# A hybrid encoder step: last tiles' squares summed by TensorE, middle r chain moved ahead, spreads inside a product, one entry's high part moved

## The chip, the cores and the metric

One core of a Trainium2 chip runs the whole step. The metric is the device time of one execution in microseconds (us); lower is better. Engine names below: PE is TensorE, DVE is VectorE, ACT is ScalarE, POOL is GpSimd, SP is SyncE, which issues nearly all DMAs.

## The reference

One step of a two-layer streaming encoder on 1,024 prompt frames and 32 sample frames (1,056 columns in all), with a model width of 1,024.

```python
def rmsnorm(x, g):
    xf = x.astype(jnp.float32)
    y = xf * lax.rsqrt(jnp.mean(xf * xf, axis=-1, keepdims=True) + EPS)
    return (y * g.astype(jnp.float32)).astype(x.dtype)
...
    for l in range(DEPTH):                       # DEPTH = 2
        h = rmsnorm(x, norm_mix[l])
        ...                                      # mixer A/B (l = 0) or mixer C (l = 1)
        x = x + y
        h = rmsnorm(x, norm_ffn[l])
        y, pf = conv_ffn(h, past_f[l], w_up[l], conv_f_w[l], w_down[l])
        new_f.append(pf)
        x = x + y
    return rmsnorm(x, norm_final), ...
```

What matters here is rmsnorm: each frame's mean square over 1,024 channels gives a factor r = (mean square + EPS)^(-1/2), which multiplies that frame's column.

## The kernel before

**Layout.** Activations lie transposed: x is 8 tiles of 128 channels by 1,056 frames (x_t[:, m, :], m = 0 to 7). So a sum over channels is a sum over 8 tiles and then over 128 partitions. Every fp32 product is made of three fp32r matmuls (split_product, lines 694 to 696): weights and activations are each split into a high part (a copy rounded by ACT) and a low part (the difference, made by POOL for weights and by DVE for activations).

**Stages.** After the first mixer come stages p = 1, 2, 3 (FFN, mixer C, FFN). A stage starts while the down products of the one before still end (last_down(p) on ACT, DVE and POOL): tile by tile x gets its residual (DVE), is scaled and split, and squared. The stage's first product is first_pair(p). It uses weight entries of 128 x 512: entries 0 and 1 for its first group (weights(0), weights(1)), 2 and 3 later. Each entry needs its high part from ACT (entry_hi, line 1417) and then its low part from POOL (entry_lo, line 1191). The products run on unnormalised x; r is applied to results. The r chain is: squares summed over tiles (sumsq), 128 partitions summed by PE against a column of ones (rms_stats), mean square on DVE (lines 1948, 1949), the power -1/2 on POOL (r_col, line 1220), spread over partitions by PE as transposes of a broadcast column (rms_spread, line 766), copied to r_rows by ACT (line 1673).

**The end.** The last down product (unit LAST) is cut into 3 chunks of columns: 0 to 400, 400 to 800 and 800 to 1,056. In each, PE makes 8 tiles of 6 matmuls. DVE adds each to x (chunk_add, line 2565), ACT squares it (end_squares_of, line 1859), and the squares are summed: chunk 0 by POOL and DVE, chunks 1 and 2 by DVE one tile at a time in PSUM (part_squares, line 2595), the last sum being written to sumsq. chunk_stats sums partitions (line 1125), chunk_mean_square (line 2572), chunk_r on POOL (line 1369), chunk_spread (line 1136) and copy_r (line 1841) follow, for chunks 0 and 1 amid the products of the next chunk. chunk_y multiplies a tile of x by r: on POOL (line 1378) in the order of POOL_Y, on DVE (line 2584) in the order of DVE_Y. Chunk 2 goes out untransposed instead: its 8 tiles are turned by PE (line 1172, 16 transposes, 2 for each tile) and scaled by r_col as they leave PSUM, half by ACT (line 1884) and half by DVE (line 2626). Both engines' halves wait for end_turned, which the last transpose raises.

**Order.** Every engine runs a list written out by hand, with waits on semaphores. SP issues the stores in the order of Y_STORES: (c, first, end) is tiles first to end - 1 of chunk c (200 KB a tile), ("act", t) and ("dve", t) are the quarters of chunk 2 (256 KB each). A store waits for its data, and all stores behind it wait too.

## Time and profile before

| | us |
|---|---|
| median of 3 runs (2094.25 to 2094.81) | 2094.79 |
| the profiled execution, its own time | 2094.42 |
| its span | 2092.6 |
| PE busy | 2080.4 |
| DVE, POOL, ACT busy | 1509.2, 964.5, 747.1 |

The profile counts time from the start of its span; 1.8 us of the execution's own time lie outside the span. Busy times overlap between engines, and a busy PE can hold matmuls that are pipelined into one another: a matmul's listed length is longer than the distance to the next one's start. Lost PE time is therefore read from start to start.

### The profile page before, as it was taken

The numbers are of one execution on the slowest core, as the hardware profiler recorded it, in microseconds if no ns is written. First come the engines' busy times: TensorE is split into PE (matmuls) and PEld (weight loads), VectorE is DVE, ScalarE is ACT, GpSimd is POOL, SyncE is SP. The second block draws the span as 40 slices with busy tenths as digits, with TensorE's granted clock in tenths as the row PEclk, the third lists the DMA queues.
The fourth block names the chain that finished last, engine by engine and source line by source line (L and its number), as shares of the span: only waits on it lengthen the run. The fifth ranks groups of instructions, "written<-read, shape, count | busy, mean of one in ns | idle before, by whom it ended". The sixth has DMA issues, their size and how long they took to land.

```text
span 2092.6 us, 36500 instructions
## 1 busy us (share of the span) xinstructions
PE 2080.4 (99%) x15414; PEld 2072.4 (99%) x15414; DVE 1509.2 (72%) x1843; ACT 747.1 (36%) x1158; POOL 964.5 (46%) x610
## 2 busy tenths in 40 slices
PE   9999999999999999999999999999999999999998
PEld 9999999999999999999999999999999999999998
DVE  6999689766666667666987677798676666766666
ACT  6574354233222322223532223453322233222234
POOL 3867335444443444443565345455444344444344
PEclk9999999999999999999999999999999999999999
DMA  4111211111111110111111111111111111011112
GB/s 167 52 33 68 99 61 42 61 61 41 41 54 49 62 51 31 61 41 61 41 41 62 41 61 41 61 41 61 41 41 61 41 61 51 31 61 42 61 43 89
DMA packets 34036, 115.66 MB, mean 55 GB/s; under 512 B 3985, under 2 KB 6545, under 8 KB 33873
## 3 DMA queue, kind: packets, MB, share of 16 engines
q1 hardware_dynamic: 33728, 112.78, 16.1%
q8 instruction: 122, 2.00, 0.4%
q10 hardware_dynamic: 144, 0.54, 0.1%
q14 instruction: 42, 0.34, 0.1%
HBM read 108.69 MB, written 4.62 MB: 54 GB/s over the span
## 4 chain that ended last, share of the span: by engine, by line
PE 93%; DVE 3%; issue 1%; POOL 1%; ACT 0%; DMA 0%; POOLq 0%; DVEq 0%; ACTq 0%
PE psum L694 31%; PE psum L696 31%; PE psum L695 30%; DVE xs_lo L1969 1%; DVE xs_lo L2209 1%; DVE work L2247 1%; DVE r_rows L2236 1%; POOL x L1378 0%; PE psum L823 0%; DVE work L2249 0%; DVE x L1936 0%; PE psum L766 0%; POOL r_col L1220 0%; DMA raw<-slabs 0%; PE psum L848 0%
## 5 line engine op out<-in xcount | busy, mean ns | idle before, releaser
L694 PE MATMUL psum<-xs_hi,w_hi 128*128 128x264 f32 (+2 forms) x3784 | 1101.5, 291 | 1.1 <-POOL w_lo L1191 0.5
L696 PE MATMUL psum<-xs_hi,w_lo 128*128 128x264 f32 (+2 forms) x3784 | 1100.0, 291 | 0.0
L695 PE MATMUL psum<-xs_lo,w_hi 128*128 128x264 f32 (+2 forms) x3784 | 1096.4, 290 | 0.0
L1191 POOL TENSOR_TENSOR w_lo<-raw,w_hi 128x512 fp32r<-128x512 f32 (+1 forms) x412 | 663.9, 1623 | 822.8 <-ACT w_hi L1417 740.5
L694 PEld LDWEIGHTS psum<-xs_hi,w_hi 128*128 128x128 f32 x3784 | 711.8, 188 | 3.3 <-issue 1.3
L695 PEld LDWEIGHTS psum<-xs_lo,w_hi 128*128 128x128 f32 x3784 | 711.3, 188 | 0.0
L696 PEld LDWEIGHTS psum<-xs_hi,w_lo 128*128 128x128 f32 x3784 | 711.2, 188 | 0.0
L694 PE MATMUL psum<-act_hi,w_hi 128*128 128x352 f32 x1200 | 388.3, 324 | 0.1
L696 PE MATMUL psum<-act_hi,w_lo 128*128 128x352 f32 x1200 | 388.2, 323 | 0.0
L695 PE MATMUL psum<-act_lo,w_hi 128*128 128x352 f32 x1200 | 385.4, 321 | 0.0
L1417 ACT ACTIVATE w_hi<-raw 128x512 fp32r<-128x512 f32 x383 | 234.0, 625 | 289.6 <-PE psum L696 268.8
L1933 DVE TENSOR_TENSOR x<-psum,x 128x704 f32<-128x704 f32 x200 | 177.8, 889 | 148.7 <-PE psum L696 143.4
L695 PEld LDWEIGHTS psum<-act_lo,w_hi 128*128 128x128 f32 x1200 | 227.4, 190 | 0.0
L694 PEld LDWEIGHTS psum<-act_hi,w_hi 128*128 128x128 f32 x1200 | 225.0, 188 | 1.1 <-issue 0.7
L696 PEld LDWEIGHTS psum<-act_hi,w_lo 128*128 128x128 f32 x1200 | 224.9, 187 | 0.0
L1965 DVE SCALAR_TENSOR_TENSOR work<-work,const 128x1058 f32<-128x1058 f32 x104 | 165.7, 1593 | 2.3
L1198 POOL TENSOR_TENSOR w_lo<-raw,w_hi 128x512 fp32r<-128x512 f32 x44 | 68.0, 1545 | 164.5 <-ACT w_hi L1404 164.5
L1706 ACT ACTIVATE work<-work 128x1024 f32<-128x1024 f32 x41 | 43.6, 1063 | 193.3 <-DVE work L1965 193.3
L1404 ACT ACTIVATE w_hi<-raw 128x1024 fp32r<-128x1024 f32 x52 | 55.1, 1059 | 160.5 <-PE psum L696 160.5
L1698 ACT ACTIVATE act_hi<-work 128x1056 fp32r<-128x1056 f32 x40 | 43.3, 1082 | 189.1 <-PE psum L696 189.1
L2444 DVE TENSOR_TENSOR work<-psum,work 128x528 f32<-128x528 f32 x53 | 37.4, 705 | 96.7 <-PE psum L696 96.7
L1936 DVE TENSOR_TENSOR x<-psum,x 128x352 f32<-128x352 f32 x200 | 102.5, 513 | 0.0
(242 smaller groups left out, 1851.0 us busy)
## 6 DMA issues: line engine op xcount, KB each, us to landing
raw<-slabs SPq DMA_DIRECT2D x186, 512.0 KB, 3.3
x<-x_t SPq DMA_DIRECT2D x15, 528.0 KB, 6.0
y_t<-x SPq DMA_DIRECT2D x4, 400.0 KB, 2.9
y_t<-x SPq DMA_DIRECT2D x8, 200.0 KB, 2.1
raw<-slabs SPq DMA_DIRECT2D x4, 256.0 KB, 8.2
y_end<-y_rows SPq DMA_DIRECT2D x4, 256.0 KB, 2.9
x<-x_t ACTq DMA_DIRECT2D x1, 528.0 KB, 4.7
x<-mix SPq DMA_DIRECT2D x1, 512.0 KB, 3.4
```

The source lines that it names most:

```text
L694: nc.tensor.matmul(out, w_hi[:, w], hi, start=start, stop=False, skip_group_check=reopen)
L695: nc.tensor.matmul(out, w_hi[:, w], lo, start=False, stop=False, skip_group_check=reopen)
L696: return nc.tensor.matmul(out, w_lo[:, w], hi, start=False, stop=stop, skip_group_check=reopen)
L1191: nc.gpsimd.tensor_tensor(w_lo[:, slab], src, w_hi[:, slab].bitcast(F32), ALU.subtract).then_inc(weights_ready, 1)
L1198: nc.gpsimd.tensor_tensor(w_lo[:, a], src[:, 0:ENTRY], w_hi[:, a].bitcast(F32), ALU.subtract)
L1404: nc.scalar.activation(w_hi[:, ring(p, unit, i)], raw_at(n), ACT.Copy).then_inc(weights_hi, 1)
L1417: nc.scalar.activation(w_hi[:, ring(p, unit, i)], entry(p, b, q, i), ACT.Copy).then_inc(weights_hi, 1)
L1698: nc.scalar.activation(ah[slot], prod[q], ACT.Copy).then_inc(act_hi_ready, 1)
L1706: nc.scalar.activation(f[:, 0:SEQ], conv_out[:, 0:SEQ], ACT.Silu)
L1933: first = dve.tensor_tensor(wide(x_t[:, m, :]), wide_banks(pset), wide(x_t[:, m, :]), ALU.add)
L1936: dve.tensor_tensor(x_t[:, m, chunk(2)], rest_bank(pset), x_t[:, m, chunk(2)], ALU.add).then_inc(tile_evacuated, 1)
L1965: dve.scalar_tensor_tensor(out, conv_in[:, k:k + GAP_COLS], cst(w_name, w_at + k), out, ALU.mult, ALU.add).then_inc(conv_tap, 1)
```

## The change

Four edits, and a new order of stores:

1. **Last tiles' squares.** In chunk 2, DVE adds up the squares of tiles 0 to 3 alone (END_SUMMED = 4), in place of all 8. PE sums the partitions of that total and then of the squares of tiles 4, 5, 6 and 7, accumulating all five in the same two PSUM columns (end_stats). The transposes of tile 0 come between tile 6's and tile 7's sums, and the other transposes after them. end_turned is now raised twice, after tile 3 (for ACT) and after tile 7 (for DVE).
2. **Middle part's r chain.** In chunk 1, DVE takes the mean square ahead of a sum of squares. POOL takes chunk 1's r after 6 tiles of y in place of 7, and chunk 2's r after 10 in place of 11. PE spreads chunk 1's r before tile 5 of chunk 2 in place of tile 6. ACT copies it before tile 4's square in place of tile 5's. DVE makes its first two tiles of y between the last additions.
3. **Spreads within a product.** rms_spread stands 3 matmuls later, inside the product that followed it, in stages 1 to 3. chunk_spread(0) stands 3 matmuls later too, between the two halves of chunk 1's tile 4.
4. **One entry's high part.** In stage 1, ACT makes entry 0's high part before tile 5's scaled copy in place of after its square, apart from entry 1's.

```diff
-Y_STORES = ((0, 4, 6), (0, 6, KD), (0, 0, 2), (0, 2, 3), (0, 3, 4), (1, 4, 5), (1, 0, 1), (1, 5, 6), (1, 1, 3), (1, 6, 7),
-            (1, 3, 4), ("act", 0), ("act", 1), ("dve", 0), (1, 7, KD), ("dve", 1))
+Y_STORES = ((0, 4, 6), (0, 6, KD), (0, 0, 2), (0, 2, 3), (1, 0, 1), (0, 3, 4), (1, 4, 5), (1, 1, 2), (1, 5, 6), (1, 2, 3),
+            (1, 3, 4), ("act", 0), (1, 6, 7), ("dve", 0), ("act", 1), ("dve", 1), (1, 7, KD))
+END_SUMMED = 4
...
                 pe.wait_ge(part_copied, 3 * n + 3)
+                block_product(a22, X_B22, x_bank, 0, False, False, halves=(0,))
                 rms_spread(p, psum[:, Y_BANK, 300:300 + ROW_REST])
-                for kp in range(KP):
+                block_product(a22, X_B22, x_bank, 0, False, False, halves=(1,))
+                for kp in range(1, KP):
                     last = block_product(a22, X_B22, x_bank, kp, False, kp == KP - 1)
...
+            def end_stats(squares, opens, closes):
+                for t, (at, rows) in enumerate(FINAL_ROWS[2]):
+                    n = 8 + t
+                    last = nc.tensor.matmul(psum[0:rows, 7, n:n + 1], squares[:, at:at + rows],
+                                            one[:], start=opens and t == 0, stop=closes, skip_group_check=True)
+                return last
...
-                    if c and m == (4, 6)[c - 1]:
-                        chunk_spread(c - 1)
+                    if (c, m) == (2, 5):
+                        chunk_spread(1)
...
+                        if (c, m, k) == (1, 4, 1):
+                            chunk_spread(0)
...
-            last.then_inc(end_turned, 1)
-            chunk_stats(2)
+            pe.wait_ge(part_summed, KD - 1 + END_SUMMED - 1)
+            end_stats(sumsq, True, False)
+            for m in range(END_SUMMED, KD - 1):
+                pe.wait_ge(square_ready, KD * 6 + m + 1)
+                end_stats(end_square[m], False, False)
+            pe.wait_ge(tile_evacuated, FINAL_EVAC + 2 * KD + 6)
+            end_turn(0)
+            pe.wait_ge(square_ready, KD * 7)
+            end_stats(end_square[KD - 1], False, True).then_inc(stats_ready, 1)
+            for m in (1, 2):
+                end_turn(m)
+            end_turn(3).then_inc(end_turned, 1)
+            pe.wait_ge(tile_evacuated, FINAL_EVAC + 3 * KD)
+            for m in (4, 5, 6):
+                end_turn(m)
+            end_turn(7).then_inc(end_turned, 1)
...
             chunk_r(0)
-            chunk_y(0, 7)
+            chunk_y(0, 6)
             chunk_r(1)
-            chunk_y(7, 11)
+            chunk_y(6, 10)
             chunk_r(2)
-            chunk_y(11, len(POOL_Y))
+            chunk_y(10, len(POOL_Y))
...
+                    if p == 1 and m == 5:
+                        entry_hi(p, 0, 0, 0)
...
-                    if m == 5:
+                    if m == 5 and p == 1:
+                        entry_hi(p, 0, 0, 1)
+                    elif m == 5:
                         entry_hi(p, 0, 0, 0, 1)
...
             for m in range(KD):
-                if m == 5:
+                if m == 4:
                     copy_r(1)
                 end_squares_of(2, m)
-                if m in (2, 4):
-                    scale(1, 5 + m // 2)
-                elif m in (0, 1, 3, 5):
-                    end_scale((m + 1) // 2)
+                if m == 2:
+                    scale(1, 6)
+                elif m in (0, 1, 3, 4):
+                    end_scale(m if m < 2 else m - 1)
+            scale(1, 7)
...
                 if m == 0:
                     part_squares(1, KD - 1)
-                elif m >= 2:
-                    part_squares(2, m - 1)
-                if m == 2:
+                elif m == 2:
                     chunk_mean_square(1)
-            part_squares(2, KD - 1)
-            chunk_y(1, 0, 1)
+                    part_squares(2, 1)
+                elif m == 4:
+                    part_squares(2, 2)
+                    chunk_y(1, 0, 1)
+                elif m == 5:
+                    part_squares(2, 3)
+            chunk_y(1, 1, 2)
             chunk_mean_square(2)
-            chunk_y(1, 1, 4)
-            dve.wait_ge(end_turned, 1)
+            chunk_y(1, 2, 4)
+            dve.wait_ge(end_turned, 2)
```

How the order of instructions moves, at three places (line numbers of the changed kernel are a little higher).

PE at the end of the program, before: after the last product (L696) stand 16 transposes of x (L1172; 4 of the 8 pairs shown) and then the partition sums of sumsq (here named r_rows, which shares its buffer; one is the column of ones).

```order
L696 MATMUL psum<-xs_hi,w_lo 128x256
L1172 MATMUL psum<-ident,x 128x128 [waits tile_evacuated,end_scaled]
L1172 MATMUL psum<-ident,x 128x128
...
L1172 MATMUL psum<-ident,x 128x128 [waits tile_evacuated]
L1172 MATMUL psum<-ident,x 128x128
L1125 MATMUL psum<-one,r_rows 128x1 [waits part_summed]
L1125 MATMUL psum<-one,r_rows 128x1
```

PE at the same place, in the changed kernel (L1135 is end_stats, L1146 the transposes):

```order
L697 MATMUL psum<-xs_hi,w_lo 128x256
L1135 MATMUL psum<-one,r_rows 128x1 [waits part_summed]
L1135 MATMUL psum<-one,r_rows 128x1
L1135 MATMUL psum<-one,end_squares 128x1 [waits square_ready]
L1135 MATMUL psum<-one,end_squares 128x1
...
L1146 MATMUL psum<-ident,x 128x128 [waits end_scaled,tile_evacuated]
L1146 MATMUL psum<-ident,x 128x128
L1135 MATMUL psum<-one,end_squares 128x1 [waits square_ready]
L1135 MATMUL psum<-one,end_squares 128x1
L1146 MATMUL psum<-ident,x 128x128 [waits end_scaled]
...
L1146 MATMUL psum<-ident,x 128x128 [waits tile_evacuated]
```

Two sums and 16 transposes became ten sums, of which eight come before any transpose, two transposes, the last two sums, and 14 transposes.

DVE in chunk 2, before, from the third addition (L2565) on; L2595 is a sum of squares, L2572 a mean square, L2584 a tile of y:

```order
L2565 TENSOR_TENSOR x<-psum,x 128x256 [waits tile_evacuated,tile_done] x2
L2595 TENSOR_TENSOR psum<-psum,end_squares 128x256 [waits square_ready]
L2572 TENSOR_SCALAR mean_sq<-psum 100x4 [waits stats_ready]
L2565 TENSOR_TENSOR x<-psum,x 128x256 [waits tile_evacuated,tile_done]
...
L2595 TENSOR_TENSOR r_rows<-psum,end_squares 128x256 [waits part_summed,square_ready]
L2584 SCALAR_TENSOR_TENSOR x<-x,const,psum 128x400 [waits r_ready,r_spread]
L2572 TENSOR_SCALAR mean_sq<-psum 128x2 [waits stats_ready]
L2584 SCALAR_TENSOR_TENSOR x<-x,const,psum 128x400 [waits r_ready,r_spread]
```

DVE at the same place, in the changed kernel (L2595 is now the addition, L2625 a sum of squares, L2602 a mean square, L2614 a tile of y):

```order
L2595 TENSOR_TENSOR x<-psum,x 128x256 [waits tile_evacuated,tile_done] x2
L2602 TENSOR_SCALAR mean_sq<-psum 100x4 [waits stats_ready]
L2625 TENSOR_TENSOR psum<-psum,end_squares 128x256 [waits square_ready]
L2595 TENSOR_TENSOR x<-psum,x 128x256 [waits tile_evacuated,tile_done] x2
L2625 TENSOR_TENSOR psum<-psum,end_squares 128x256 [waits part_summed,square_ready]
L2614 SCALAR_TENSOR_TENSOR x<-x,const,psum 128x400 [waits r_ready,r_spread]
L2595 TENSOR_TENSOR x<-psum,x 128x256 [waits tile_evacuated,tile_done]
L2625 TENSOR_TENSOR r_rows<-psum,end_squares 128x256 [waits part_summed,square_ready]
L2595 TENSOR_TENSOR x<-psum,x 128x256 [waits tile_evacuated,tile_done] x2
L2614 SCALAR_TENSOR_TENSOR x<-x,const,psum 128x400 [waits r_ready,r_spread]
L2602 TENSOR_SCALAR mean_sq<-psum 128x2 [waits stats_ready]
```

Seven sums of squares became three; the first tile of y stands before the last three additions and the second right behind them.

## Rows read from the trace of the kernel before

**Rows 1.** The page, busy time of each engine.
```profile
PE 2080.4 (99%) x15414; PEld 2072.4 (99%) x15414; DVE 1509.2 (72%) x1843; ACT 747.1 (36%) x1158; POOL 964.5 (46%) x610
```

**Rows 2.** Busy time by stage: us, each engine's busy time, PEclk, DMA share, GB/s.
```profile
2082.00:2093.00 11.00, 2.07 (x19) 1.87 (x17) 4.96 (x11) 2.10 (x5) 4.18 (x5) 0.71 0.67 250
```

**Rows 3.** Timeline of PE: spreads of stages 1 and 3 (start, us).
```profile
333.18 0.28 PE L696 MATMUL psum<-xs_hi,w_lo 128*128 128x264 f32 x1
333.63 1.23 PE L766 MATMUL psum<-ident,r_col 128*128 128x128 f32 x9 [0.18 <-POOL r_col L1220]
...
1389.86 0.28 PE L696 MATMUL psum<-xs_hi,w_lo 128*128 128x264 f32 x1
1390.34 1.23 PE L766 MATMUL psum<-ident,r_col 128*128 128x128 f32 x9 [0.20 <-POOL r_col L1220]
```

**Rows 4.** Timeline of POOL ahead of stage 1's spread.
```profile
329.67 1.58 POOL L1305 TENSOR_TENSOR xs_lo<-work,xs_hi 128x528 fp32r<-128x528 f32 x1 [4.45 <-ACT xs_hi L1654]
331.22 2.27 POOL L1220 TENSOR_TENSOR r_col<-mean_sq,minus_half 128x9 f32<-128x9 f32 x1
```

**Rows 5.** Timeline of PE, POOL, ACT and DVE where stage 1 starts.
```profile
309.92 0.32 PE L696 MATMUL psum<-xs_hi,w_lo 128*128 128x352 f32 x1
310.74 0.36 PE L694 MATMUL psum<-xs_hi,w_hi 128*128 128x264 f32 x1 [0.49 <-POOL w_lo L1191]
...
307.32 3.16 POOL L1191 TENSOR_TENSOR w_lo<-raw,w_hi 128x512 fp32r<-128x512 f32 x2 [2.77 <-ACT w_hi L1417]
...
306.62 1.14 ACT L1417 ACTIVATE w_hi<-raw 128x512 fp32r<-128x512 f32 x2
...
309.23 2.36 DVE L2209 SCALAR_TENSOR_TENSOR xs_lo<-x,const,xs_hi 128x1056 fp32r<-128x1056 f32 x1
```

**Rows 6.** Timeline of PE in the last two chunks and behind.
```profile
2069.41 0.34 PE L696 MATMUL psum<-xs_hi,w_lo 128*128 128x400 f32 x1
2069.90 0.56 PE L1136 MATMUL psum<-ident,r_col 100*128 100x100 f32 x4
...
2081.68 1.91 PE L1172 MATMUL psum<-ident,x 128*128 128x128 f32 x16
2083.47 0.61 PE L1125 MATMUL psum<-one,r_rows 128*128 128x1 f32 x4
```

**Rows 7.** Timeline of DVE behind chunk 1's products.
```profile
2078.49 0.15 DVE L2572 TENSOR_SCALAR mean_sq<-psum 100x4 f32<-100x4 f32 x1
...
2082.09 0.41 DVE L2565 TENSOR_TENSOR x<-psum,x 128x256 f32<-128x256 f32 x1
...
2084.11 0.16 DVE L2572 TENSOR_SCALAR mean_sq<-psum 128x2 f32<-128x2 f32 x1 [0.16 <-PE psum L1125]
2084.19 1.71 DVE L2584 SCALAR_TENSOR_TENSOR x<-x,const,psum 128x400 f32<-128x400 f32 x3
```

**Rows 8.** Timeline of ACT and POOL in the same stretch.
```profile
2080.92 0.48 ACT L1841 ACTIVATE r_rows<-psum 128x400 f32<-128x400 f32 x1
...
2071.07 7.12 POOL L1378 TENSOR_TENSOR x<-x,r_rows 128x400 f32<-128x400 f32 x7 [1.23 <-ACT r_rows L1841]
2078.72 1.01 POOL L1369 TENSOR_TENSOR r_col<-mean_sq,minus_half 128x4 f32<-128x4 f32 x1 [0.52 <-DVE mean_sq L2572]
...
2081.48 3.04 POOL L1378 TENSOR_TENSOR x<-x,r_rows 128x400 f32<-128x400 f32 x3 [0.74 <-ACT r_rows L1841]
2084.46 0.72 POOL L1369 TENSOR_TENSOR r_col<-mean_sq,minus_half 128x2 f32<-128x2 f32 x1
```

**Rows 9.** Timeline of SP's queue: stores (1, 1, 3) and ("dve", 1).
```profile
2085.39 0.38 SPq L685 DMA_DIRECT2D y_t<-x  x1
...
2089.34 0.64 SPq L676 DMA_DIRECT2D y_end<-y_rows  x1
```

**Rows 10.** Busy time in quarters of a us; the last two columns are DMA share and GB/s.
```profile
2086.25:2086.50 0.25, 0.00 (x0) 0.00 (x0) 0.25 (x2) 0.25 (x1) 0.00 (x0) 1.00 0.78 294
...
2091.50:2091.75 0.25, 0.00 (x0) 0.00 (x0) 0.00 (x0) 0.00 (x0) 0.00 (x0) 0.50 0.85 328
```

More of the change, by code:

```diff
@@ L924, in _, with block_product @@
                 last.then_inc(tile_done, 1)
[L926 to L928 removed]
+            def block_product(slab, which, first_bank, kp, opens, closes, reopen=False, halves=(0, 1)):
+                for h in halves:
                     at = kp * KP_COLS + which + h * PART
@@ L1127, in chunk_stats, with end_turn @@
                 last.then_inc(stats_ready, 1)
+            def end_stats(squares, opens, closes):
[4 more added lines that the diff above has]
+                return last
+            def end_turn(m):
+                if m < 4:
+                    pe.wait_ge(end_scaled, m + 1)
+                    bank = END_BANKS["act"]
+                else:
+                    bank = END_BANKS["dve"]
+                for t in range(END_ROWS):
+                    last = nc.tensor.transpose(psum[:, bank[t], m % 4 * P:(m % 4 + 1) * P],
+                                               x_t[:, m, END + t * P:END + (t + 1) * P], ident[:])
+                return last
             def chunk_spread(c):
```

18 lines of the change are left out of this document (2 added, 16 removed).

## The prediction, made before the changed kernel ran

> **What bounds the kernel now.** I read the page first: PE is busy for 2080.4 of 2092.6 us [rows 1], so all that any change off PE can win is 12.2 us. I then went through PE's timeline for places where one matmul starts later than the usual distance behind the last. Inside the program these are few and small. At each of the three spreads of r the first transpose starts 0.45 to 0.48 us behind a matmul whose followers come every 0.12 us [rows 3]; that is 0.33 us lost in stage 1 and 0.36 in stage 3, and 0.27 in stage 2, the one of the three not shown. Stage 1's first product starts 0.66 us late (0.82 us behind the last one, where 0.16 is usual), put down to a weight's low part on POOL [rows 5]. The spread of chunk 0 starts 0.49 us behind, where 0.18 is usual: 0.31 us lost [rows 6].
>
> The rest lies behind the last product, where PE is busy 2.07 of 11 us [rows 2]. There I asked what ends last. It is the stores: the DMA engines move 294 GB/s from 2086.25 on, are nearly full from then (the last quarter of a microsecond still has 328), and stop before 2091.75 [rows 10]. By the shares of those two quarters (0.78, 0.85) data flow from 2086.27 to 2091.71. SP issued the store that opens this stretch at 2085.39 [rows 9], 0.88 us before its data move. From it to the last there are 400 + 200 + 200 + 256 + 256 + 256 + 200 + 256 = 2,024 KB = 2.073 MB, in 5.44 us: 381 GB/s. The span ends 0.89 us later. So the end is not a chain of engines but a full DMA path, and the rule that I use is: the end is, over all stores, the latest of (issue + 0.88 + bytes from this store on / 381 GB/s), plus 0.89. What counts is how early the data before the last ones leave, not when the last tile is ready.
>
> **The spreads within a product.** Three matmuls at 0.12 us are put ahead of each rms_spread: 0.36 us of cover. What the spread waits for is r_col, which POOL ends at 331.22 + 2.27 = 333.49 [rows 4]; the transposes begin 0.14 us behind. Nothing in the edit moves r_col, so the spread stays where it is and the three matmuls are won: 0.33, 0.27 and 0.36, which is 0.96 us. Behind the spread ACT copies r as before, and PE comes to the next pair 0.36 us earlier with no wait listed there. If r_col were later by some d, as much would be lost again; if all cover came to nothing, the term is 0. I take -0.96.
>
> **The moved entry.** Before, ACT makes both high parts from 306.62 on and POOL both low parts from 307.32 to 310.48, 1.2 to 1.6 us each [rows 5]. The high part of entry 0 (0.57 us) now falls in a gap of ACT. POOL could make its low part up to 2.7 us earlier. Yet I count nothing for it, for two reasons. First, what the 0.66 us win, the spread gives back: r_col of stage 1 stands behind POOL's xs_lo at 329.67, which had waited 4.45 us for ACT [rows 4]; ACT in turn waited for DVE, whose list has no gap from the start of stage 1 to there. PE would only wait longer at the spread. Second, DVE and POOL hinder each other. The DVE row at 309.23 ends 2.36 us later, at 311.59, 1.11 us behind POOL's two [rows 5]: as if it had stood still until POOL was through, for 1.25 us. So each of POOL's subtractions can push DVE's chain, and with it r_col, by about that. Before, one does. After, by the order of requests the total may be the same (0), and at worst both do: 1.25 us later. I take 0, and keep 0 to +1.3.
>
> The Trainium skill, "SBUF — State Buffer", section "Who interferes with whom", says that a DVE instruction with two SBUF inputs and a GpSimd instruction that reads SBUF exclude each other for the whole length of whichever issued first. The row of 2.36 us agrees. By that rule alone an earlier POOL subtraction would come ahead of DVE's and hold it up, which is the first rival below.
>
> **The last chunks, PE and DVE up to the additions.** Times are on the clock of before; only differences inside the end count. chunk_spread(0) costs no wait any more: PE is 0.31 us earlier from there on, and DVE, which follows it tile by tile, too. Chunk 1's r: its stats end near 2077.4. The mean square then stands first on DVE (2077.45, for 2078.49 [rows 7]). POOL has ended six tiles by then (seven took 7.12 us, so 1.02 each [rows 8]), and r_col lasts 1.01 from 2077.7. So r is there at 2078.7 for 2079.73, PE spreads before tile 5, and ACT's copy starts at 2079.8 for 2080.92 [rows 8], where its list now comes to it. r_rows is ready at 2080.3 for 2081.4. DVE's first y waits for that (2080.31), and holds up the additions of tiles 5 to 7. From 2080.31 on DVE is full: 0.55 to the next instruction behind a y, 0.34 behind an addition or a sum. So tile 5's addition starts at 2080.86, the last sum of squares at 2081.20, tile 6's and 7's additions at 2081.55 and 2081.9, the last for 2082.09 [rows 7]. The two lost waits and the one new one nearly cancel.
>
> **PE's sums.** The total of tiles 0 to 3 is written at 2081.63 on DVE (2081.20 + 0.43). A sum is four records on PE's timeline, where two matmuls stand in the program [rows 6]. From 2083.47 those four take 0.61, of which 0.25 is the last one's own length, so 0.12 a record; 16 transposes in 1.91 are 0.11 each. Nine of ten matmuls now read squares that are already there, so PE runs at its own pace: 20 records x 0.11 + 2 x 0.11 for tile 0's transposes, from 2081.69 on, is 2084.1, and the last result 0.2 later. The mean square of chunk 2 starts at 2084.3 for 2084.11 [rows 7]. So this edit takes four additions (0.35 each) and a wait from DVE, but puts 2.4 us of PE into the chain, and r of chunk 2 is not earlier: 2085.25 for 2085.18 [rows 8]. The six transposes of tiles 1 to 3 end before that, those of tiles 4 to 7 at 2085.8: ACT writes its quarters as before, DVE too (2085.87, for 2085.82 which is 0.08 before the end of its y [rows 7]).
>
> **y and the stores.** POOL after r: chunk 0's last two to 2080.7, chunk 1's tiles 4 and 5 end at 2081.75 and 2082.75 (before, 2082.5 and 2083.5 [rows 8]). It then waits for chunk 2's mean square until 2084.5, and ends tile 6 at 2086.3 and tile 7 at 2087.3, the latter 1.1 us later than before. DVE ends tiles 0 and 1 at 2080.95 and 2082.85, and, behind the mean square (2084.4), tile 2 at 2085.0 and tile 3 at 2085.55 (three of them in 1.71, so 0.62 each and 0.55 apart [rows 7]). SP's last wait before the path fills is tile 2 of chunk 1: issued at 2085.03, with 200 + 200 + 256 + 200 + 256 + 256 + 256 + 200 = 1,824 KB = 1.868 MB from there on. 2085.03 + 0.88 + 4.90 = 2090.81. Tile 3: 2085.58 + 0.88 + 4.36 = 2090.82. ("act", 0): 2086.06 + 0.88 + 3.83 = 2090.77. Tile 7, though last and late, is issued long after it is ready. Data end at 2090.82 for 2091.71: -0.89 us.
>
> The Trainium skill, "DMA: Bandwidth & Descriptors", section "Where 436 GB/s comes from", puts transfers between HBM and SBUF at about 358 GB/s. The trace shows 381 with one core running, and the measurement decides; by 358 the same two sums would be 5.79 and 5.22 us of data, and the term -0.93 instead of -0.89.
>
> **Sum.** -0.96 (spreads) + 0 (entry) - 0.89 (stores) = -1.85 us. PE's 0.31 us of chunk 0 is inside the second. Against the profiled execution: 2094.42 - 1.85 = 2092.57. The median of the runs shown is 0.37 above it: 2094.79 - 1.85 = 2092.9.
>
> **Rivals.** A measurement of this kernel tells about 0.2% (4.2 us) from no change; of faster and slower in that sense nearly nothing is in reach, since all of PE's losses in the program are 2.1 us and the end's can't fall below its bytes.
> - *The moved entry delays r of stage 1.* DVE is blocked by both subtractions: +1.3 on r_col, so stage 1 gives +1.0 in place of -0.33. Time: 2092.9 + 1.3 = 2094.2. For it: the row of 2.36 us. Against: POOL asks back to back, and the two are likelier to take the same slots as before. 0.08.
> - *The stores win nothing.* POOL's idle 1.8 us before r of chunk 2, or DVE's y behind PE's sums, moves the opening store back: 2085.03 becomes 2085.9. Only the spreads are left: 2094.79 - 0.96 = 2093.8. 0.14.
> - *The spreads win nothing,* as the wait comes back at another place, or the switch between transposes and product was the gap: 2094.79 - 0.89 = 2093.9. For it: the profile itself puts only 0.18 and 0.20 of the gaps down to r_col [rows 3]. 0.07.
> - *Slower.* Ten sums in a row into the same two PSUM columns no longer pipeline. Every 0.1 us more per record adds 2.0 us ahead of chunk 2's mean square and of DVE's tiles 2 and 3, thus to the end. At 0.20 a record the store term is +0.9 and cancels the spreads; at 0.25 (a record's whole length) it is -0.89 + 2.8 = +1.9, and the kernel takes 2094.79 - 0.96 + 1.9 = 2095.7. Against: the four records of before already add into the same columns at 0.12. 0.05.
> - *More than forecast.* The sums go faster than DVE's old chain, or the copy of r finds ACT free earlier, and the opening store leaves 0.6 to 1.2 us earlier: 2091.7 to 2092.3. 0.12.
> - *As forecast,* within 0.7 us: 0.54.
>
> **The numbers.** All cases but part of the slower one and of the last lie between 2091.4 and 2094.6; this leaves out under 0.2 even with the runs' own spread (0.56 us). 0.2% below is 2090.6: I give it 0.04, as losses of 4.2 us are hardly there to be won. 0.2% above is 2099.0: 0.02. Within: 0.94.
>
> **What would show it.** In the changed trace: the spreads start within 0.2 us of their neighbours, at the same distance behind r_col, and each stage is about 0.3 us earlier; the first product of stage 1 starts late as before or the spread waits longer; the mean square of chunk 2 at the same distance from the last product as before or a little more; POOL idle for over 1 us before chunk 2's r; data end 0.9 us nearer to PE's last product plus 0.3. Wrong would be: a DVE chain in stage 1 that is longer by over a microsecond, a record of the sums over 0.15 us, or a DMA path that is not full in the last 4 us.

## The result and the profile after

| | us |
|---|---|
| before, median of 19 runs (2094.05 to 2095.35) | 2094.52 |
| changed, median of 19 runs (2097.01 to 2099.71) | 2097.98 |
| ratio, 95% interval | 1.0017 (1.0011 to 1.0023) |
| profiled execution, its span | 2095.6 (before 2092.6) |

The kernel is 3.5 us slower, outside the range of the prediction (2091.4 to 2094.6), though within the 0.2% that it had called the bound of no change. The page of the changed kernel, its line of busy times:

```profile
PE 2082.2 (99%) x15430; PEld 2073.8 (99%) x15430; DVE 1511.7 (72%) x1839; ACT 747.0 (36%) x1158; POOL 967.1 (46%) x610
```

Against [rows 1] that says nothing: a stall of 1 us drowns in it. What tells is the distance from one matmul's start to the next on PE's timeline. In the changed kernel it shows a later start of stage 1, and three waits that the kernel before does not have, one in each stage, 19 to 31 us behind the spread of r. PE of the changed kernel at the start of stage 1, at its spread, and at the three waits:

```profile
309.94 0.32 PE L697 MATMUL psum<-xs_hi,w_lo 128*128 128x352 f32 x1
311.59 0.39 PE L695 MATMUL psum<-xs_hi,w_hi 128*128 128x264 f32 x1 [1.33 <-DVE x L1966]
...
334.42 0.28 PE L697 MATMUL psum<-xs_hi,w_lo 128*128 128x264 f32 x1
334.72 1.25 PE L767 MATMUL psum<-ident,r_col 128*128 128x128 f32 x9
...
353.00 0.29 PE L697 MATMUL psum<-xs_hi,w_lo 128*128 128x264 f32 x1
354.36 0.39 PE L695 MATMUL psum<-xs_hi,w_hi 128*128 128x264 f32 x1 [1.08 <-ACT work L1799]
...
1077.89 0.28 PE L697 MATMUL psum<-xs_hi,w_lo 128*128 128x264 f32 x1
1078.69 0.39 PE L695 MATMUL psum<-xs_hi,w_hi 128*128 128x264 f32 x1 [0.52 <-ACT work L1769]
...
1411.25 0.29 PE L697 MATMUL psum<-xs_hi,w_lo 128*128 128x264 f32 x1
1412.52 0.39 PE L695 MATMUL psum<-xs_hi,w_hi 128*128 128x264 f32 x1 [0.99 <-ACT work L1799]
```

The first product starts 0.85 us later than in [rows 5] (311.59 for 310.74), the spread 1.09 us later than in [rows 3] (334.72 for 333.63). The spread itself no longer waits much (0.30 us behind its neighbour for 0.45). Then come starts 1.36, 0.80 and 1.27 us apart where 0.12 is usual. The spreads of stages 2 and 3 start at 1047.56 and 1393.00, for 1045.42 and 1390.34 before: the loss grows from stage to stage. From the start of the last product (2084.70, before 2081.56) to the span's end it is 10.90 us for 11.04, so nearly nothing is won at the end.

Why stage 1 starts late, in the changed kernel: POOL (L1216 are the low parts of entries 0 and 1), and DVE from tile 5 on:

```profile
304.53 2.31 POOL L1216 TENSOR_TENSOR w_lo<-raw,w_hi 128x512 fp32r<-128x512 f32 x1
307.34 1.84 POOL L1216 TENSOR_TENSOR w_lo<-raw,w_hi 128x512 fp32r<-128x512 f32 x1 [0.49 <-ACT w_hi L1442]
...
305.61 2.42 DVE L1999 TENSOR_TENSOR xs_lo<-work,xs_hi 128x528 fp32r<-128x528 f32 x2
307.96 2.35 DVE L2266 TENSOR_TENSOR r_rows<-r_rows,work 128x1056 f32<-128x1056 f32 x1
310.23 0.88 DVE L1963 TENSOR_TENSOR x<-psum,x 128x704 f32<-128x704 f32 x1
311.03 0.51 DVE L1966 TENSOR_TENSOR x<-psum,x 128x352 f32<-128x352 f32 x1
311.46 1.30 DVE L2239 SCALAR_TENSOR_TENSOR xs_lo<-x,const,xs_hi 128x1056 fp32r<-128x1056 f32 x1
```

ACT's high part did fall into its gap (303.28), and POOL's low part starts 2.8 us earlier. But now both of POOL's subtractions fall on DVE instructions that read and write SBUF: L1999 takes 2.42 us and L2266 2.35. In the kernel before, the same two took 1.31 and 1.25, and one instruction alone was held up, the 2.36 us of [rows 5], which is now free at 1.30. Two blocks of about 1.1 us for one: DVE reaches the addition of tile 6 (L1963) 2.2 us later, PE waits for it, and r_col comes 1.17 us later (POOL starts on it at 332.39, for the 331.22 of [rows 4]).

### The profile page after: what moved, and what is told of

It is laid out like the page before. It is cut to its first block, busy times and chain, and to the rows that moved or that the text cites. A ratio compares the mean times of both kernels' runs of the same rounds, so it can differ in the third digit from the quotient of the medians.

```text
span 2095.6 us, 36523 instructions
## 1 busy us (share of the span) xinstructions
PE 2082.2 (99%) x15430; PEld 2073.8 (99%) x15430; DVE 1511.7 (72%) x1839; ACT 747.0 (36%) x1158; POOL 967.1 (46%) x610
## 4 chain that ended last, share of the span: by engine, by line
PE 88%; DVE 8%; issue 2%; POOL 1%; ACT 1%; DMA 0%; SPq 0%; DVEq 0%; ACTq 0%
PE psum L695 29%; PE psum L697 29%; PE psum L696 29%; DVE xs_lo L1999 2%; DVE xs_lo L2239 1%; DVE work L2277 1%; DVE r_rows L2266 1%; DVE work L1995 1%; DVE work L2279 0%; DVE x L1966 0%; PE psum L824 0%; DMA x<-x_t 0%; POOL r_col L1245 0%; DVE raw L2230 0%; POOL xs_lo L1330 0%
## 5 line engine op out<-in xcount | busy, mean ns | idle before, releaser
L696 PE MATMUL psum<-xs_lo,w_hi 128*128 128x264 f32 (+2 forms) x3784 | 1096.2, 290 | 0.0
L1216 POOL TENSOR_TENSOR w_lo<-raw,w_hi 128x512 fp32r<-128x512 f32 (+1 forms) x412 | 666.2, 1630 | 823.8 <-ACT w_hi L1442 741.7
L696 PEld LDWEIGHTS psum<-xs_lo,w_hi 128*128 128x128 f32 x3784 | 711.3, 188 | 0.0
L696 PE MATMUL psum<-act_lo,w_hi 128*128 128x352 f32 x1200 | 385.4, 321 | 0.0
L1963 DVE TENSOR_TENSOR x<-psum,x 128x704 f32<-128x704 f32 x200 | 177.8, 889 | 148.5 <-PE psum L697 143.3
L696 PEld LDWEIGHTS psum<-act_lo,w_hi 128*128 128x128 f32 x1200 | 227.4, 189 | 0.0
```

What stands on the lines that cost most here:

```text
L696: nc.tensor.matmul(out, w_hi[:, w], lo, start=False, stop=False, skip_group_check=reopen)
L1216: nc.gpsimd.tensor_tensor(w_lo[:, slab], src, w_hi[:, slab].bitcast(F32), ALU.subtract).then_inc(weights_ready, 1)
L1963: first = dve.tensor_tensor(wide(x_t[:, m, :]), wide_banks(pset), wide(x_t[:, m, :]), ALU.add)
```

## The experiments

Twelve kernels, and then, since the tail was still open, two more and four further executions of two of them. Every median stands beside the kernel before on the same chip: k_spread, k_entry, k_tail and k_noentry beside 2094.64; k_spread_swap, k_spread_silu, k_entry_late and k_r_early beside 2094.43; k_after_swap, k_after_fix, k_tail_stores and k_best beside 2094.40; the last two beside 2094.63. Kernels are compared by their distances to it. Each interval of a ratio is about 0.0009 to either side, so single differences under 2 us lie inside it; I read them by medians of 11 runs, their ranges, and the traces.

### The parts alone

**k_spread.** rms_spread inside the product, and nothing else:

```diff
+                block_product(a22, X_B22, x_bank, 0, False, False, halves=(0,))
                 rms_spread(p, psum[:, Y_BANK, 300:300 + ROW_REST])
+                block_product(a22, X_B22, x_bank, 0, False, False, halves=(1,))
-                for kp in range(KP):
+                for kp in range(1, KP):
```

> The kernel before with rms_spread inside the product (edit 3's first half) alone. Theory A: as forecast, the three spreads lose their waits, -0.96 us, 2093.5, and no wait of over 0.5 us behind any of them. Theory B: the copy of r and PE's second pair shift against DVE and POOL, and PE waits about 1 us for ACT's copy of a result in each stage, 353.0, 1077.9 and 1411.2 on the clock of the changed kernel: 3 waits of 0.5 to 1.2 us less the 0.96 won, thus 2095 to 2096.5.

Measured: 2097.06 (2096.75 to 2097.54), +2.42. Theory A, my forecast, falls, and the loss is larger than theory B's too; the largest part of the whole loss is here. DVE and POOL of this kernel behind the spread of stage 1:

```profile
337.83 1.22 DVE L2309 TENSOR_TENSOR work<-work,r_rows 128x1024 f32<-128x1024 f32 x1
338.97 1.28 DVE L2311 TENSOR_TENSOR work<-work,r_rows 128x32 f32<-128x32 f32 x1
340.17 1.31 DVE L2314 TENSOR_TENSOR work<-psum,r_rows 128x528 f32<-128x528 f32 x2
341.40 5.84 DVE L1971 TENSOR_TENSOR xs_lo<-slots_hi,xs_hi 128x528 fp32r<-128x528 f32 x4
...
338.68 1.53 POOL L1193 TENSOR_TENSOR w_lo<-raw,w_hi 128x512 fp32r<-128x512 f32 x1 [2.11 <-ACT w_hi L1419]
341.33 3.02 POOL L1193 TENSOR_TENSOR w_lo<-raw,w_hi 128x512 fp32r<-128x512 f32 x2 [1.13 <-ACT w_hi L1419]
```

The same engines in the kernel before:

```profile
338.63 0.18 DVE L2309 TENSOR_TENSOR work<-work,r_rows 128x32 f32<-128x32 f32 x1
338.73 1.32 DVE L2312 TENSOR_TENSOR work<-psum,r_rows 128x528 f32<-128x528 f32 x2
339.97 3.66 DVE L1969 TENSOR_TENSOR xs_lo<-slots_hi,xs_hi 128x528 fp32r<-128x528 f32 x4
...
338.74 1.30 POOL L1191 TENSOR_TENSOR w_lo<-raw,w_hi 128x512 fp32r<-128x512 f32 x1 [2.51 <-ACT w_hi L1417]
341.40 4.62 POOL L1191 TENSOR_TENSOR w_lo<-raw,w_hi 128x512 fp32r<-128x512 f32 x3 [1.36 <-ACT w_hi L1417]
```

Before, DVE's product of 32 columns was ahead of POOL's subtraction by 0.11 us (338.63, 338.74). PE's matmuls release the entry that ACT and then POOL take, so with PE 0.36 us nearer to the r chain POOL comes first (338.68, 338.97), and 0.18 us of work take 1.28.

The four low parts of t1 meet POOL's next subtractions, and three of the four take 1.79 us each. Before, only one of them did (1.80), but two DVE instructions behind them were held up instead, new_f (128x4, 1.26 us for 0.16) and L1961 (1.68 for 0.77); the convolution is held up once in both. Each kernel makes five POOL subtractions in this stretch; before, the first one fell on DVE instructions that read PSUM and cost nothing, here all five cost DVE 0.9 to 1.1 us. So the net loss is one block. From the 1,024-column product to the end of the convolution (L1965, there L1967) DVE needs 13.91 us (337.83 to 351.74) for 12.82 (337.50 to 350.32).

Stages 2 and 3 show the same: DVE's 32-column product was ahead of POOL by 0.10 us in each before (1050.42 for 1050.52, 1395.34 for 1395.44), is behind it now (1051.71 for 1051.56, 1397.26 for 1396.94), and takes 1.28 us both times. In stages 1 and 3 ACT's silu waits for the convolution, ACT's copy out of PSUM (L1772) stands behind silu, and PE waits for the copy; in stage 2 the copy (L1742) waits for DVE itself.

The waits account for the time. A stalled matmul starts 1.37 us behind the last for 0.12, and the one after it 0.23 for 0.12: 1.36 us in stages 1 and 3, by the same rows 0.81 in stage 2, together 3.53. Less 0.96 for the covered spreads it is +2.57; the span without what differed ahead of stage 1 (2095.5 - 0.33 - 2092.6) gives +2.57 as well.

**k_entry.** Edit 4 alone:

```diff
+                    if p == 1 and m == 5:
+                        entry_hi(p, 0, 0, 0)
                     act.wait_ge(tile_evacuated, read(m))
```

> The kernel before with edit 4 alone (entry 0's high part ahead of tile 5's scaled copy). Theory A, the moved entry starts the loss: POOL's two subtractions now hold up DVE twice for about 1.2 us where one did, so stage 1's first product starts 0.85 us later, r_col of stage 1 is 1.2 us later than before, and since the spread stands in its old place the whole of it is lost: 1.2 us, perhaps 1 more where later waits open, thus 2095.7 to 2096.7 beside a kernel before of 2094.5. Theory B, the spreads inside a product are at fault and the entry is harmless: 2094.5.

Measured: 2095.37 (2095.15 to 2095.66), +0.73. PE starts stage 1 at 311.50, and waits again at its spread, 334.72 with 0.47 us put down to r_col. Theory A's mechanism holds; the loss is smaller than the 1.2 to 2.2 us that it gave.

**k_tail.** Edits 1 and 2, the stores and chunk_spread(0).

> The kernel before with edits 1 and 2, the order of stores and chunk_spread(0) three matmuls later, but neither the moved entry nor rms_spread's new place. From the last product's start to the span's end the changed kernel took 10.9 us for 11.04: if that holds without the delays ahead of it, this gives -0.14 us, and with chunk_spread(0) -0.45: 2094.0 to 2094.4. The forecast's own term was -0.89, 2093.6. If the tail's edits carried part of the loss, it lies above 2094.8.

Measured: 2094.37 (2093.54 to 2096.12), -0.27, and 2.6 us wide for 1.0 before. The profiled execution has 2093.54, 0.88 us under that of before, which is the forecast's own number; but not all of it is the tail's. It is 0.34 us ahead already where chunk 0 begins, in front of everything that these edits touch. The first product of chunk 0 in the kernel before, and in k_tail:

```profile
2055.77 0.34 PE L694 MATMUL psum<-xs_hi,w_hi 128*128 128x400 f32 x1
```

```profile
2055.43 0.34 PE L695 MATMUL psum<-xs_hi,w_hi 128*128 128x400 f32 x1
```

From this product to the end of the span k_tail takes 36.3 us for 36.8. That distance is the measure of the tail: the six profiled kernels without any of its edits lie within 0.01 us of one another in it. So the tail gave -0.6 here, 0.4 of it ahead of the last product's start and 0.2 behind it.

**k_noentry.** The changed kernel without edit 4.

> The changed kernel with edit 4 undone. Theory A: r_col of stage 1 is back where it was, all three spreads are covered, -0.96 and the tail's -0.14 to -0.9: 2092.7 to 2093.4. Theory B: about the changed kernel's time less the 0.2 that the entry costs: 2097 to 2098.

Measured: 2097.18 (2096.27 to 2098.37). The three waits stand as in k_spread (1.08, 0.53 and 1.09 us idle; there 1.08, 0.54, 1.08). The parts nearly add: 2.42 + 0.73 - 0.27 = 2.88 of 3.5.

### Is it the race with POOL?

**k_spread_swap.** k_spread, and DVE takes the short product first:

```diff
-                dve.tensor_tensor(g[:, 2:2 + SEQ], g[:, 2:2 + SEQ], r_rows[:, 0:SEQ], ALU.mult).then_inc(tile_evacuated, 1)
                 sample = g[:, 2 + SAMPLE + GAP:2 + GAP_COLS]
                 dve.tensor_tensor(sample, sample, r_rows[:, SAMPLE:COLS], ALU.mult).then_inc(tile_evacuated, 1)
+                dve.tensor_tensor(g[:, 2:2 + SEQ], g[:, 2:2 + SEQ], r_rows[:, 0:SEQ], ALU.mult).then_inc(tile_evacuated, 1)
```

> rms_spread inside the product in stages 1 to 3, and DVE's two products with r behind it in the other order: the 32 columns first, then the 1,024. Theory P (a lost race with POOL): in the run with the spread alone, POOL's subtraction at 338.68 came ahead of the 32-column product, which took 1.28 us for 0.18, and the one at 341.33 ahead of four subtractions, which took 5.84 us for 3.66. With the long product last DVE is busy when POOL asks, so the 32 columns are not held up, DVE's chain is 1 to 2 us shorter, and PE's waits at 353.6 and 1411.9 shrink or go: 2094.3 to 2095.5 for 2097.06. Theory Q (PE is simply 0.36 us nearer to a chain that did not move): nothing changes but the order, 2097.0.

Measured: 2093.98 (2093.54 to 2094.36), 0.45 under before where k_spread is 2.42 above it. DVE and POOL of this kernel in the same place:

```profile
337.90 0.18 DVE L2310 TENSOR_TENSOR work<-work,r_rows 128x32 f32<-128x32 f32 x1
338.01 1.22 DVE L2311 TENSOR_TENSOR work<-work,r_rows 128x1024 f32<-128x1024 f32 x1
...
338.71 1.68 POOL L1193 TENSOR_TENSOR w_lo<-raw,w_hi 128x512 fp32r<-128x512 f32 x1 [2.07 <-ACT w_hi L1419]
```

POOL asks at the same moment, but DVE is amid its long instruction, so this time POOL stands (1.68 us, the longest of its first subtraction in the three kernels) and DVE's chain is 12.82 us again (337.90 to 350.72). PE's three waits are gone from the list of waits. Theory P holds: two instructions exchanged, with the same work, are worth 2.9 us. At 352.56 PE still starts 0.32 us behind its neighbour: ACT's copy starts at 351.92 and PE 0.64 later, as it did in k_spread (352.94, 353.58). By the same distance the kernel before had 0.25 us of slack there (copy at 351.51, PE on time at 352.40), less than the 0.36 won at the spread.

**k_spread_silu.** k_spread, with ACT's copy (L1770 of before) ahead of silu in stages 1 and 3:

```diff
-                if p != 2 and before == FIRST:
-                    silu_gate(p, 0, 0)
                 act.wait_ge(tile_done, group_done(p, b, q, 3))
...
                 nc.scalar.activation(two(half(up, 1)), halves_of(Z_BANK), ACT.Copy).then_inc(part_copied, 1)
+                if p != 2 and before == FIRST:
+                    silu_gate(p, 0, 0)
```

> rms_spread inside the product in stages 1 to 3, and in stages 1 and 3 ACT copies the first pair's fourth group out of PSUM before it computes silu of the first gate, in place of after. If PE's waits of 1.08 us in stages 1 and 3 (353.6, 1411.9; 1.25 from start to start) are for that copy standing behind silu, which stands behind DVE's convolution, they go, though POOL still holds up DVE: 2097.06 less 2.5 is 2094.6, of which the wait of 0.54 in stage 2 is left. If DVE or a low part is just as late, the wait stays with another name: above 2096.

Measured: 2096.44 (2096.16 to 2096.86), +2.01, so only 0.4 better than k_spread. The copy now starts at 349.51 and PE no longer waits for it, but PE stops 2.5 us later, at 356.04, idle for 0.73 us, put down to DVE (work, L2446), and likewise at 1413.84. DVE and POOL of k_spread there, and then of k_spread_silu:

```profile
353.68 0.71 DVE L2441 TENSOR_TENSOR work<-work,r_rows 128x528 f32<-128x528 f32 x1
354.13 3.68 POOL L1193 TENSOR_TENSOR w_lo<-raw,w_hi 128x512 fp32r<-128x512 f32 x2 [4.78 <-ACT w_hi L1419]
```

```profile
353.56 1.81 DVE L2441 TENSOR_TENSOR work<-work,r_rows 128x528 f32<-128x528 f32 x1
353.51 2.98 POOL L1193 TENSOR_TENSOR w_lo<-raw,w_hi 128x512 fp32r<-128x512 f32 x2 [4.28 <-ACT w_hi L1419]
```

It is the same race, lost at a new place. With its copy out of the way ACT makes the next two high parts 0.6 us earlier (352.82 for 353.43), POOL's subtraction starts 0.05 us ahead of DVE's product with r, and that product takes 1.81 us for 0.71; in stage 3 the starts are 1411.31 and 1411.36. L2446, which PE waits for, stands right behind it. Had the product taken 0.71 us, L2446 would have ended near 354.9 (an estimate: 1.1 us off its end at 355.98), ahead of PE's turn at 355.14. So the copy was rightly named as what PE waited for, and moving it moved POOL onto DVE once more.

**k_entry_late.** k_entry, with POOL's first low part held back until both high parts are there:

```diff
                 for i in entries:
+                    if (p, b, q, i) == (1, 0, 0, 0):
+                        pool.wait_ge(weights_hi, step_of(p, ("pair", b, q), 1) + 1)
                     split_lo(step_of(p, ("pair", b, q), i), ring(p, ("pair", b, q), i), entry(p, b, q, i))
```

> The kernel before with edit 4, but POOL starts entry 0's low part only when entry 1's high part is there too, as in effect before. ACT's order is that of the moved entry, POOL's times are those of before. Theory A (the loss of 0.73 us comes through POOL's early subtraction, which holds DVE up twice): back to 2094.6. Rival (ACT's own order is the cause, since tile 5's scaled copy comes 0.57 us later): 2095.4, as with edit 4 alone.

Measured: 2094.47 (2094.34 to 2094.99), +0.04. ACT's order is the moved one, only POOL's start is back at 307.26: the whole loss of edit 4 comes from POOL's early subtraction.

**k_after_swap, k_after_fix.** The same two mends in the changed kernel: first the exchange on DVE alone, then also POOL held back.

> The changed kernel with one thing else: DVE's 32-column product with r ahead of the 1,024-column one in stages 1 to 3. The lost race accounts for 3.1 us in the kernel with the spreads alone (2097.06 to 2093.98). If it is the same loss here, 2098.0 becomes 2094.9. If the moved entry's delay in stage 1 or the tail opens the waits in another way, it stays above 2096.

> The kernel of the run before with POOL's low part of entry 0 in stage 1 held back until entry 1's high part is there. Both losses are then undone with all four edits in place: 2094.9 less 0.9 (entry alone 2095.37, held back 2094.47) is 2094.0, with the width of the tail edits, 2 us and more between the fastest and the slowest. If the losses overlap, above 2094.5.

Measured, beside 2094.40: 2094.68 (2094.21 to 2095.80) and 2093.82 (2092.95 to 2094.99). Of 3.5 us lost, the exchange on DVE gives back 3.2 and the hold on POOL 0.9. With all four edits in place and these two races decided for DVE, the changed kernel is 0.6 us below before.

### The tail

**k_r_early.** Without edit 1 (DVE sums all eight squares, PE turns first and sums last), the rest of the tail kept, and the stores in the order in which their data come:

```diff
-Y_STORES = ((0, 4, 6), (0, 6, KD), (0, 0, 2), (0, 2, 3), (1, 0, 1), (0, 3, 4), (1, 4, 5), (1, 1, 2), (1, 5, 6), (1, 2, 3),
+Y_STORES = ((0, 4, 6), (0, 6, KD), (0, 0, 2), (0, 2, 3), (0, 3, 4), (1, 4, 5), (1, 5, 6), (1, 0, 1), (1, 1, 2), (1, 2, 3),
             (1, 3, 4), ("act", 0), (1, 6, 7), ("dve", 0), ("act", 1), ("dve", 1), (1, 7, KD))
...
                 elif m == 2:
                     chunk_mean_square(1)
-                    part_squares(2, 1)
-                elif m == 4:
-                    part_squares(2, 2)
-                    chunk_y(1, 0, 1)
-                elif m == 5:
-                    part_squares(2, 3)
-            chunk_y(1, 1, 2)
+                if m >= 2:
+                    part_squares(2, m - 1)
+            part_squares(2, KD - 1)
+            chunk_y(1, 0, 1)
```

> The kernel before with edit 2 (chunk 1's r earlier on DVE, POOL, PE and ACT), chunk_spread(0) three matmuls later and the stores in the order in which their data are ready, but without edit 1: DVE adds up all eight squares, PE turns the tiles first and sums last. In the run with all tail edits the stores ended 0.9 us earlier in the profiled execution, but the times lie between 2093.54 and 2096.12; in another kernel with these edits PE's granted clock fell to half while it still turned tiles, which took 3.23 us for 1.73. Theory C (PE at work 5 us behind its last product meets the fall of the clock in some executions): here PE ends 2.5 us behind it, so the times lie within 1 us of one another, at 2093.7 to 2094.2. Theory S (the new order of stores is what varies): the width stays above 1.5 us.

Measured: 2093.61 (2093.22 to 2094.10), -0.82, within 0.9 us of one another. From chunk 0's first product to the span's end it is 35.8 us for 36.8.

**k_tail_stores.** All the tail's edits, with that order of stores.

> All the tail's edits with the stores in the order in which their data are ready, the order of the run without edit 1 (2093.61, 2093.22 to 2094.10). Theory C (the wide times come from PE's sums and the clock): as wide as with the edits' own order of stores, 2093.5 to 2096, median 2094.2 to 2094.4. Theory S (the order of stores made them wide): within 1 us of one another, median near 2093.6.

Measured: 2093.99 (2093.86 to 2094.69), -0.41, narrow: theory S seemed to win. Four more executions went on from there, three of this kernel and one of k_tail.

> Another profiled execution of the tail edits with the stores in the order of their data. Theory C (the clock): where PE's granted clock falls before PE ends, about 3 us behind the start of the last product, PE ends 6.5 us behind it for 5.0 and the time is about 1 us above 2093.9; where it falls at 8 us, the time is 2093.9. Theory S (the edits' order of stores made the wide times): the span ends 10.9 us behind the last product whatever the clock does.

> The same kernel once more: does the clock fall before PE ends, and where does the span end behind the last product (10.9 us with a late fall; C: 11.8 with an early one, S: 10.9).

> The same kernel once more, for the same two numbers: the moment of the fall, and the span's end behind the last product (C: 11.8 with an early fall, S: 10.9).

> The tail edits with their own order of stores, once more (2093.54 to 2096.12 in eleven executions). C: a time near 2093.6 to 2094.3 with the clock's fall at 8 us behind the last product, or 2094.7 and more with a fall at 3 us. S: a time above 2094.7 also comes with a late fall.

Measured, one execution each beside 2095.22 of before: 2094.30, 2094.61, 2094.38 and, for look_tail_1, 2095.72. PE of look_stores_1 from its sums on, and then of look_tail_1, the same instructions in the same order:

```profile
2084.32 0.42 PE L1144 MATMUL psum<-ident,x 128*128 128x128 f32 x2
2084.57 0.50 PE L1133 MATMUL psum<-one,end_squares 128*128 128x1 f32 x4
2084.93 1.72 PE L1144 MATMUL psum<-ident,x 128*128 128x128 f32 x14
```

```profile
2084.72 0.48 PE L1144 MATMUL psum<-ident,x 128*128 128x128 f32 x2
2084.99 0.86 PE L1133 MATMUL psum<-one,end_squares 128*128 128x1 f32 x4
2085.72 3.00 PE L1144 MATMUL psum<-ident,x 128*128 128x128 f32 x14
```

Windows of look_tail_1 (us, each engine's busy time, PEclk, DMA share, GB/s):

```profile
2084.00:2085.00 1.00, 1.00 (x11) 1.00 (x10) 0.06 (x1) 0.49 (x1) 0.00 (x0) 0.97 0.81 296
2085.00:2088.00 3.00, 3.00 (x17) 3.00 (x16) 1.25 (x3) 0.73 (x2) 1.87 (x3) 0.50 0.52 194
```

The granted clock fell from 2.4 to 1.2 GHz while PE still worked, and fourteen transposes took 3.00 us for 1.72. Across the eleven profiles of kernels with edit 1 there are two cases and nothing between: the clock falls 8.0 to 8.9 us behind the start of the last product, PE ends at 5.0 and the span at 10.9 (six profiles, the changed kernel's among them), or it falls at 2.9 to 3.6, PE ends at 6.2 to 6.7 and the span at 11.4 to 11.9 (five). From chunk 0's first product the late ones take 36.3 us and the early ones 36.8 to 37.2, for 36.8 before. In the nine profiles without edit 1 the clock fell at 4.3 to 7.4, and PE had ended at 2.4 to 2.5 every time.

The fall is not the whole width. Of the 2.2 us between k_tail's profile and look_tail_1, the same kernel, 0.95 lies behind the start of the last product, and 1.23 ahead of it (2080.83, 2082.06), where nothing differs but the execution.

**k_fix_stores, k_r_early_old.** The square completed: the mended changed kernel with the stores as their data come, and k_r_early with the change's own order of stores.

> The changed kernel with both mends (32 columns first, entry 0's low part held back) and the stores in the order of their data: PE's extra sums are in, only the order of stores differs from the run that took 2093.82 (2092.95 to 2094.99). If the order of stores decides whether the clock falls amid PE's last work, all executions show the late fall and lie within 1 us of one another, near 2093.2 to 2093.5. If the looks with a late fall were chance, the width is again 2 us and the median 2093.8.

> The kernel without PE's extra sums (DVE adds all squares, PE ends 2.5 us behind the last product) but with the change's own order of stores, which blocks the queue at tile 0 of chunk 1. If the wide times need both, PE's late work and this order, the executions lie within 1 us of one another here, and the median is 2093.6 to 2094.2 (2093.61 with the stores as their data come). If the order of stores alone makes them wide, 2 us.

Measured, beside 2094.63: 2093.48 (2092.82 to 2094.94), 2.1 us wide, and its profile has the early fall (at 3.6); 2094.71 (2094.41 to 2095.23), 0.8 us wide. So the width follows edit 1 and not the order of stores: all eight kernels without edit 1 are 0.5 to 0.9 us wide in their 11 runs, and of those with it all but one are 1.6 us wide or more; k_tail_stores, narrow in 11 runs and with the late fall in 4 profiles of 4, stays unexplained beside k_fix_stores. What decides between early and late, while PE's own instructions stand at the same distances to 0.03 us, is open. Without edit 1 the change's order of stores has a price of its own, 0.9 us (+0.08 for -0.82; 37.1 us for 35.8 from chunk 0's first product), where tile 0 of chunk 1 is late: in k_r_early_old nothing is moved for 2 us. With edit 1, and a late fall, the two orders end alike (36.3). Windows of k_r_early_old:

```profile
2082.20:2083.20 1.00, 1.00 (x12) 1.00 (x11) 0.85 (x4) 0.71 (x3) 1.00 (x2) 1.00 0.00 0
2083.20:2084.20 1.00, 0.99 (x10) 0.88 (x8) 0.87 (x2) 0.39 (x1) 0.06 (x1) 1.00 0.00 0
2084.20:2085.20 1.00, 0.00 (x0) 0.00 (x0) 0.97 (x3) 0.00 (x0) 0.73 (x2) 1.00 0.25 90
```

### What helped, together

**k_best.** k_spread_swap and k_r_early in one kernel.

> What helped, together: rms_spread inside the product with the 32 columns first on DVE (2093.98 for 2094.43), chunk 1's r earlier, chunk_spread(0) inside a tile and the stores as their data come, without PE's extra sums and without the moved entry (2093.61 for 2094.43). If the two gains add: 2094.43 - 0.45 - 0.82 = 2093.2, range 2092.7 to 2093.7, faster than both kernels. If stage 2 or 3 meets another order between POOL and DVE: 2094 or more.

Measured: 2092.82 (2092.64 to 2093.39), ratio 0.9992 (0.9984 to 1.0001): 1.6 us under before, which is 5.0 better than the changed kernel, and no run of it reaches the lowest of before (2093.97). Its spread in stage 1 starts 0.12 us behind its neighbour, and its span ends 10.45 us behind the last product for 11.04:

```profile
333.59 0.28 PE L697 MATMUL psum<-xs_hi,w_lo 128*128 128x264 f32 x1
333.71 1.20 PE L767 MATMUL psum<-ident,r_col 128*128 128x128 f32 x9
...
2080.55 0.28 PE L697 MATMUL psum<-xs_hi,w_lo 128*128 128x256 f32 x1
2080.67 1.91 PE L1195 MATMUL psum<-ident,x 128*128 128x128 f32 x16
```

## Why the prediction was wrong

**The spreads (-0.96; measured +2.42).** This is the step that failed, and in one sentence of it: "PE comes to the next pair 0.36 us earlier with no wait listed there." The spreads were covered as forecast. But that no wait is listed says that the chain there is in time, not by how much, and the slack was 0.25 us. Worse, I took all other engines' times as fixed. POOL's subtractions follow PE (each needs a slot that PE has released), so they came earlier against DVE's list, overtook an instruction that had led by 0.11 us, and the DVE chain grew by 1.1 us. I had written of this exclusion for the moved entry, and did not look for it behind the spreads. The rival "the spreads win nothing" named the right kind of place and put its price at 0.

The Trainium skill, "SBUF — State Buffer", section "Who interferes with whom", calls the pair of ports that DVE and GpSimd share an exclusive lock, held for the length of the instruction that has it. The runs agree: 0.18 us of work took 1.28 and 0.69 took 1.79, each 1.1 us longer and ending with the POOL subtraction (1.30 us by itself) or behind it; instructions of DVE that read PSUM took 0.70 beside it, as without it.

**The moved entry (0, range 0 to +1.3; measured +0.73 alone, 0.9 within the change).** The rival, given 0.08, is what happened: both subtractions block DVE, r_col is 1.17 us late where I wrote 1.3. The argument against it ("the two are likelier to take the same slots as before") was a guess about which of two comes first, and the trace could have settled it: POOL free at 304.6, DVE's list without a gap, so that each early subtraction had to fall on something. The bounds were right, the choice between them not.

**The last chunks and the stores (-0.89 with chunk_spread(0); measured -0.27).** This term was mis-sized twice. First, it is -0.6 even where the clock falls late. In k_tail's profile most of the forecast's times came out to 0.05 us, chunk 2's mean square at 2084.30 (forecast 2084.3), and that is luck: the execution was 0.34 us ahead before the tail began. Against its own last product the mean square starts 3.47 us behind; the forecast's times make that 3.05 (2084.3 less 2081.25, which is 2081.56 - 0.31). The step that failed is DVE's first y, which I let start as soon as r_rows is copied (2080.31 behind 2080.3). ACT's copy and DVE's y in k_tail:

```profile
2079.40 0.48 ACT L1864 ACTIVATE r_rows<-psum 128x400 f32<-128x400 f32 x1
...
2080.35 0.63 DVE L2608 SCALAR_TENSOR_TENSOR x<-x,const,psum 128x400 f32<-128x400 f32 x1 [1.02 <-ACT r_rows L1864]
```

The copy ends where I had it, 0.95 us ahead of the last product, and y starts 0.47 us later, in every profile with edit 1 by 0.45 to 0.47; the sums, the mean square and the stores follow. What fills that time is open. Second, in five of eleven profiles PE's clock falls amid its last work, and the tail wins nothing or loses up to 0.4 us: PE ends 5.0 us behind the last product in place of 2.5, and the early fall costs 0.5 to 1.0 us at the end of the span. I had read the clock's column in the last rows of before [rows 2, 10] without asking where it would stand against a longer list on PE. The sums themselves ran at 0.11 us a record, as taken; the rival of slower sums did not come.

**Edit 1 itself** cost time even so: with one order of stores k_tail_stores is at -0.41 and k_r_early without it at -0.82, and with a late fall the tail takes 36.3 us with it and 35.8 without. I had worked out that r of chunk 2 is not earlier by it (2085.25 for 2085.18); what the edit buys is free time on DVE, which nobody at the end needed.

## What to carry to other kernels

When an edit brings one engine forward, ask which instructions of other engines follow it, and against which list they then move; where DVE and POOL both work in SBUF, compare the starts of the two within a microsecond, and put DVE's short instructions of a critical chain ahead of its long one, where POOL will ask. A wait that isn't listed has an unknown slack, not an unlimited one: work it out from the releaser's time before a gain is carried past it. Nor does it help by itself to move the named releaser: look first what the move brings forward. And work moved to PE behind the last large product is priced twice, at either level of the clock.

## What the runs showed that was not expected

- The order of two independent DVE products of 1,024 and 32 columns decides 2.9 us in 2,094 (3.2 in the changed kernel): each of three stages loses 0.8 to 1.4 us when POOL comes between them.
- PE's granted clock falls after the last product at a moment that differs between executions of the same instructions, 2.9 to 8.9 us behind its start. Ahead of each of the five early falls PE had made at least its first 16 one-column records of sums (1.9 us) and the two transposes of tile 0; in the six late ones it had made the same by then, so this does not tell them apart.
- The releaser named for PE's wait (an ACT copy) was right, and moving it did not help: with the copy 3.4 us earlier POOL came 0.05 us ahead of a DVE product, and PE stopped 2.5 us further on.
- Without the tail's edits the stretch from chunk 0's first product to the span's end repeats to 0.01 us in six kernels; what differs by over a microsecond between executions of one kernel lies ahead of it. A tail is better measured from such a point than by the whole time.
